# The last output product of a three-layer kernel, by token tiles instead of column blocks

## The chip, the cores and the metric

The kernel runs on one core of one Trainium2 chip. The metric is the device time of one execution in microseconds (us). TensorE multiplies matrices, VectorE and ScalarE do elementwise work, GpSimd helps with both, and SyncE issues the transfers. "Clock" below is the clock granted to TensorE.

## What is computed

A hidden state of 512 tokens x 1024 channels goes through a gated linear attention layer with an MLP, a differential attention layer with an MLP, and a third layer with two mixers side by side. The part that changes is the end of the third layer:

```python
y = jnp.einsum('bsc,cd->bsd', jnp.concatenate([o_a.astype(x.dtype), o_b], axis=-1), w_o[layer])
x = _layer_norm(DEEPNORM_ALPHA * x + y, ln_g[layer], ln_b[layer])

def _layer_norm(x, g, b):
    xf = x.astype(jnp.float32)
    mu = jnp.mean(xf, axis=-1, keepdims=True)
    var = jnp.mean(jnp.square(xf - mu), axis=-1, keepdims=True)
    y = (xf - mu) * lax.rsqrt(var + LN_EPS) * g.astype(jnp.float32) + b.astype(jnp.float32)
```

Here w_o is 1024 x 1024, the mean is over the 1024 channels of one token, and everything is float32. o_a comes from four attention heads (each gated by `a_gate`), o_b from four heads of a recurrence (gated by `b_gate`).

## The kernel before, in words

The state lives channel-major: `X[:, j, :]` holds channels 128j to 128j+127 on the partitions and all 512 tokens along the row. A product is split in two parts for accuracy: a value becomes a rounded high part and the rest, its low part (`Hh`/`Hl` for inputs, `Oh`/`Ol` for what goes into an output product, `Wh`/`Wl` for weights), and a product is three matmuls: high x high, low x high, high x low.

Weights stream through in 231 blocks, each 1024 inputs x 128 output columns, 512 KB. For each block b SyncE loads a raw tile (`weights`, three raw buffers, so b waits until the low part of b - 3 is done), ScalarE copies it rounded into a slot of `WH` (`w_hi`, line 1024 of the profile), VectorE subtracts (`w_lo`, line 1561), and TensorE runs 8 x 3 matmuls with the block as stationary and 512 tokens as moving operand (`add_k`, lines 483, 484, 486) into one PSUM bank. The blocks use three slots in turn; a block's copy waits for the product that last used its slot.

Each engine has one program in a fixed order. Around the change:

- Blocks 193 to 222 (`TWO` + n, n = 0 to 29) project the third layer's inputs. After block n each engine runs `two_tick(n)`, the steps of the attention heads and the recurrence that are due, up to n = 37. On TensorE, ticks 31 to 37 stand between the k steps of the output product. Lines of these ticks that matter here: 539 (transposes of 128 x 128), 942 (attention weights times values), 965 (value projection), 1113 to 1120 on ScalarE and 1648 on VectorE (the gate's silu), 2057 (gating of a head), 1103 and 1643 (high and low part of O).
- Blocks 223 to 230 (`TWO_WO` + j) are w_o. 223 and 224 are built together, one k after the other as the parts of O become ready (order `KORDER_2`: the recurrence's heads first), then the other six one by one. They alternate between PSUM banks 0 and 1.
- VectorE adds each block to the residual (line 2114), GpSimd sums the blocks over j (2206, 2209).
- Then the layer norm: mean by two products with a matrix of ones (lines 1003, 1005), centring on VectorE (2120), squares on ScalarE (1544), the variance by eight products with ones (1010), `rstd` on ScalarE (1047, 1049), scaling on VectorE (2123), bias on ScalarE (1548), and eight stores of 256 KB from SyncE (464).

`TB` and `G456` are rings of PSUM banks (2, 3 and 4, 5, 6); `take` hands out the next bank with the event that frees it. In `CB` lie the recurrence's states in this stage, in `con` the constants.

## Time and profile before

| | |
|---|---|
| median of 3 runs | 1589.82 us (1588.62 to 1593.27) |
| the profiled execution | 1588.16 us, of which the span of the records 1586.8 us |
| TensorE busy | 1533.2 us (97%), 7486 matmuls |
| VectorE, ScalarE, GpSimd busy | 993.5, 670.6, 174.1 us |
| mean granted clock | 0.99 of full |

"Busy" adds the records of an engine, so an engine that is busy 97% of the time is not the bound everywhere; the chain that ended last tells for each stretch who was waited for. The records of matmuls overlap: a matmul's duration is longer than the distance to the next one, and the distance (called pitch below) is what a stream of them costs. A few per cent of the matmul records can be missing.

### The profile page before, as it was taken

What the parts mean: (1) busy time and instruction counts of PE and PEld (TensorE: products, weight loads), DVE (VectorE), ACT (ScalarE), POOL (GpSimd) and SP (SyncE); (2) the same over time, 40 slices, a digit from 0 to 9 for tenths busy, and PEclk for the clock granted to TensorE, in tenths of its full rate; (3) what the DMA queues carried; (4) which work ended last, traced back from release to release, by engine and by line L of the source; (5) the groups of instructions that cost most, each with busy time, mean ns of one, the idle gap of its engine ahead of it and who ended that gap; (6) DMA issues with size and microseconds to landing.
All of it is one profiled execution on the core that took longest, in us unless ns stands there. A gap on an engine that the chain in (4) does not pass through costs nothing.

```text
span 1586.8 us, 18855 instructions
## 1 busy us (share of the span) xinstructions
PE 1533.2 (97%) x7486; PEld 1246.1 (79%) x7486; DVE 993.5 (63%) x1588; ACT 670.6 (42%) x1126; POOL 174.1 (11%) x160
## 2 busy tenths in 40 slices
PE   9999999999999999999988999999999999999997
PEld 6777878888888888777766878888888866887774
DVE  7476667866666655777774643434344569997743
ACT  6454434513232334465554532324133455555633
POOL 0000002000000001111102100000001003664110
PEclk9998999999999999999999999999999999999999
DMA  9234445565656542222212343333333122212111
GB/s 370 102 129 132 125 142 168 168 215 190 197 186 204 188 127 81 69 64 67 67 54 67 106 113 93 104 96 93 97 97 99 48 83 80 67 40 80 41 53 53
DMA packets 52172, 180.79 MB, mean 114 GB/s; under 512 B 5762, under 2 KB 6658, under 8 KB 52083
## 3 DMA queue, kind: packets, MB, share of 16 engines
q1 hardware_dynamic: 52082, 179.57, 36.0%
q8 instruction: 59, 0.97, 0.3%
q14 instruction: 31, 0.25, 0.0%
HBM read 176.01 MB, written 3.41 MB: 113 GB/s over the span
## 4 chain that ended last, share of the span: by engine, by line
PE 82%; DVE 8%; ACT 5%; POOL 2%; DMA 1%; issue 1%; SPq 1%; DVEq 0%; ACTq 0%
PE PS L483 22%; PE PS L486 22%; PE PS L484 22%; PE PS L493 2%; PE PS L494 2%; PE PS L496 2%; PE PS L720 1%; DVE sb_Wl L1561 1%; PE PS L539 1%; PE PS L869 1%; PE PS L739 1%; POOL sb_TMD L2194 1%; ACT sb_Wh L1024 1%; PE PS L633 1%; DMA sb_rg<-ada 1%
## 5 line engine op out<-in xcount | busy, mean ns | idle before, releaser
L483 PE MATMUL PS<-sb_Hh,sb_Wh 128*128 128x512 f32 (+1 forms) x1016 | 405.8, 399 | 2.3 <-DVE sb_Hl L1592 2.3
L486 PE MATMUL PS<-sb_Hh,sb_Wl 128*128 128x512 f32 (+1 forms) x1016 | 396.5, 390 | 0.6 <-DVE sb_Wl L1561 0.6
L484 PE MATMUL PS<-sb_Hl,sb_Wh 128*128 128x512 f32 (+1 forms) x1016 | 396.6, 390 | 0.0
L1024 ACT ACTIVATE sb_Wh<-sb_RAW 128x1024 fp32r<-128x1024 f32 x223 | 233.7, 1049 | 317.5 <-PE PS L486 310.1
L1561 DVE TENSOR_TENSOR sb_Wl<-sb_RAW,sb_Wh 128x1024 fp32r<-128x1024 f32 x223 | 282.2, 1266 | 94.0 <-ACT sb_Wh L1024 94.0
L483 PE MATMUL PS<-sb_Oh,sb_Wh 128*128 128x512 f32 x672 | 265.3, 395 | 5.5 <-DVE sb_X L1632 1.9
L486 PE MATMUL PS<-sb_Oh,sb_Wl 128*128 128x512 f32 x672 | 262.7, 391 | 2.7 <-DVE sb_Wl L1561 2.7
L484 PE MATMUL PS<-sb_Ol,sb_Wh 128*128 128x512 f32 x672 | 262.4, 391 | 0.0
L483 PEld LDWEIGHTS PS<-sb_Hh,sb_Wh 128*128 128x128 f32 (+1 forms) x1016 | 190.2, 187 | 59.1 <-issue 15.8
L486 PEld LDWEIGHTS PS<-sb_Hh,sb_Wl 128*128 128x128 f32 (+1 forms) x1016 | 190.2, 187 | 43.1 <-DVE sb_Wl L1561 1.0
L484 PEld LDWEIGHTS PS<-sb_Hl,sb_Wh 128*128 128x128 f32 (+1 forms) x1016 | 190.4, 187 | 39.9 <-issue 1.0
L1632 DVE SCALAR_TENSOR_TENSOR sb_X<-PS,sb_MOD,sb_X 128x512 f32<-128x512 f32 x76 | 57.0, 750 | 165.0 <-PE PS L486 165.0
L483 PEld LDWEIGHTS PS<-sb_Oh,sb_Wh 128*128 128x128 f32 x672 | 126.7, 189 | 33.7 <-ACT sb_Wh L1024 2.2
L486 PEld LDWEIGHTS PS<-sb_Oh,sb_Wl 128*128 128x128 f32 x672 | 126.7, 189 | 29.7 <-DVE sb_Wl L1561 3.2
L484 PEld LDWEIGHTS PS<-sb_Ol,sb_Wh 128*128 128x128 f32 x672 | 126.8, 189 | 26.6 <-issue 0.7
L2135 POOL TENSOR_TENSOR sb_SSQ<-sb_SSQ,sb_TMA 128x512 f32<-128x512 f32 x24 | 42.9, 1786 | 781.6 <-ACT sb_TMA L1039 781.6
L1792 DVE TENSOR_TENSOR sb_TMD<-sb_TMA 128x512 f32<-128x512 f32 x64 | 44.3, 692 | 121.3 <-ACT sb_TMA L1242 121.3
L1242 ACT ACTIVATE sb_TMA<-PS 128x512 f32<-128x512 f32 x64 | 38.1, 596 | 193.1 <-PE PS L486 188.0
L1568 DVE CUSTOM_DVE_ANT_0 sb_ARW<-sb_ARW,sb_CB,sb_vec 128x1024 f32<-128x1024 f32 x86 | 115.0, 1340 | 0.2
L1643 DVE TENSOR_TENSOR sb_Ol<-sb_TMD,sb_Oh 128x512 fp32r<-128x512 f32 x68 | 47.1, 693 | 2.9 <-DVE sb_TMD L1792 0.4
L1299 ACT ACTIVATE sb_WK<-PS,sb_st 128x512 f32<-128x512 f32 (+3 forms) x64 | 33.0, 525 | 33.1 <-DVE sb_st L1878 33.1
L493 PE MATMUL PS<-sb_Hh,sb_Wh 128*128 128x256 f32 x128 | 37.2, 290 | 6.3 <-DVE sb_Hl L1613 4.9
(355 smaller groups left out, 1942.7 us busy)
## 6 DMA issues: line engine op xcount, KB each, us to landing
sb_RAW<-w SPq DMA_DIRECT2D x128, 512.0 KB, 3.6
sb_ARW<-ada SPq DMA_DIRECT2D x86, 512.0 KB, 4.5
sb_RAW<-diff_in SPq DMA_DIRECT2D x24, 512.0 KB, 3.6
sb_RAW<-gla_in SPq DMA_DIRECT2D x20, 512.0 KB, 3.7
sb_RAW<-in_b SPq DMA_DIRECT2D x16, 512.0 KB, 4.0
sb_RAW<-gla_wo SPq DMA_DIRECT2D x8, 512.0 KB, 3.6
sb_RAW<-diff_wo SPq DMA_DIRECT2D x8, 512.0 KB, 3.6
sb_RAW<-wo SPq DMA_DIRECT2D x8, 512.0 KB, 3.6
```

What stands on the lines that cost most here:

```text
L483: mm(to[0:m, :], WH[si][:, k, 0:m], hi[:, k, :], start=first, stop=False)
L484: mm(to[0:m, :], WH[si][:, k, 0:m], lo[:, k, :], start=False, stop=False)
L486: ins = mm(to[0:m, :], WL[si][:, k, 0:m], hi[:, k, :], start=False, stop=last)
L493: mm(to, WH[si][:, k, :], hi[:, k, ts], start=k == 0, stop=False)
L1024: act(WH[slot_of(b)][:, :, 0:m], RAWS[raw_of(b)][:, 0:8 * m].rearrange("p (k m) -> p k m", k=8), ACT.Copy).then_inc(*done("w_hi", b))
L1242: act(to, bank(b), ACT.Relu).then_inc(*done("evac_a", b))
L1561: tt(WL[si][:, :, 0:m], RAWS[raw_of(b)][:, 0:8 * m].rearrange("p (k m) -> p k m", k=8), WH[si][:, :, 0:m].bitcast(F), ALU.subtract).then_i ...
L1568: e.op.tensor_tensor_reduce(w, w, CB[:], 1.0, V("ada_b", layer * 48 + t), ALU.mult, ALU.add, col).then_inc(*done("mod", layer, t))
L1632: stt(X[:, j, :], bank(b), gates_of[first][:, j:j + 1], X[:, j, :], ALU.mult, ALU.add).then_inc(*done("evac_d", b))
L1643: tt(Ol[:, k, :], src, Oh[:, k, :].bitcast(F), ALU.subtract).then_inc(*done("o_lo", stage, k))
L1792: tt(q, r, r, ALU.mult).then_inc(*done("m_sq", b))
L2135: tt(SSQ[:], SSQ[:], TA.buf(("sq", i, j)), ALU.add).then_inc(*done("ssq", i, j))
```

## The change

The last output product is computed token-major. For a tile i of 128 tokens and a half f of 512 output columns, a PSUM bank first gets the residual, by four transposes of `X`, and then 8 x 3 matmuls are added to it, with the tile's columns of `Oh`/`Ol` as stationary operand and four weight blocks (4 x 128 columns) as moving operand. (0, 0) and (1, 0) are built together between ticks 31 to 37, then (2, 0), (3, 0), (0, 1), (1, 1), (2, 1), (3, 1), each in a bank of its own. Since the residual isn't multiplied any more, O is divided by `ALPHA` instead, through the value weights and the recurrence's gain, and the norm's epsilon by its square.

All eight blocks of w_o are held at once: 223 to 225 in the three slots, 226 in a fourth slot over `CB` and the first 1024 columns of `con`, 227 to 230 over `Hh`/`Hl`. 226 is converted after block 221 (n = 28), 227 to 230 after the last tick.

The norm runs per token tile: VectorE takes statistics of each half (`bn_stats`), merges them, and makes two passes for each half; ScalarE computes the reciprocal root of one column. The gain and bias, now along the row, are loaded to all partitions. GpSimd has no part in it. Stores are 128 tokens x 512 columns. The output tensor is token-major.

```diff
@@ -155,16 +155,20 @@
+    if b >= TWO_WO + 3:
+        return b - TWO_WO + 6
     return THIRD.get(b, b if b < FIRST else (b - sum(b > n for n in THIRD)) % 3)
...
 BANKS[DIFF_WO + 2] = 4
-BANK = [BANKS.get(b, "turns" if b in THIRD or b in FOURTH else b % 2) for b in range(BLOCKS)]
+BANK = [BANKS.get(b, "turns" if b in THIRD or b in FOURTH else b % 2) for b in range(TWO_WO)]
 SLOT_BEFORE, BANK_BEFORE, NEXT_WEIGHTS = {}, {}, {}
-for _b in range(FIRST, BLOCKS):
+for _b in range(FIRST, TWO_WO + 3):
     SLOT_BEFORE[_b] = max(n for n in range(_b) if _b in THIRD or slot_of(n) == slot_of(_b))
-    BANK_BEFORE[_b] = max((n for n in range(_b) if BANK[n] == BANK[_b]), default=None)
+    if _b < TWO_WO:
+        BANK_BEFORE[_b] = max((n for n in range(_b) if BANK[n] == BANK[_b]), default=None)
@@ -249,22 +252,29 @@
-        Wh, Wl = sb("Wh", [P, 3, 8, 128], R), sb("Wl", [P, 3, 8, 128], R)
+        with ExitStack() as place:
+            Wh = sb("Wh", [P, 4, 8, 128], R, place)
+        sb("three_of_Wh", [P, 3072])
+        CB = sb("CB", [P, 1024])
+        with ExitStack() as place:
+            Wl = sb("Wl", [P, 4, 8, 128], R, place)
+        sb("three_of_Wl", [P, 3072])
+        con = sb("con", [P, NCON])
         RAW = sb("RAW", [P, 3, 1024])
         vec = sb("vec", [P, NVEC])
-        con = sb("con", [P, NCON])
         ones = sb("ones", [P, 128])
...
         epsb = sb("epsb", [P, 2])
-        CB = sb("CB", [P, 1024])
         relb = sb("relb", [32, 4])
...
         TMD = sb("TMD", [P, 2, T])
+        hgs = sb("hgs", [P, 4])
+        lst, lmv = sb("lst", [P, 4, 12]), sb("lmv", [P, 4, 4])
@@ -304,6 +314,8 @@
+        WH += [Wh[:, 3]] + [OV(Hh, n) for n in range(4)]
+        WL += [Wl[:, 3]] + [OV(Hl, n) for n in range(4)]
@@ -314,6 +326,8 @@
+        rows_bank = lambda i, f: [PS[:, 1, :], G456.buf(("out", 0, 1)), PS[:, 0, :], PS[:, 7, :], G456.buf(("out", 2, 0)),
+                                  TB.buf(("out", 2, 1)), G456.buf(("out", 3, 0)), TB.buf(("out", 3, 1))][2 * i + f]
@@ -350,6 +364,9 @@
+        TOK = [slice(i * 128, (i + 1) * 128) for i in range(4)]
+        LNG, LNB = SEL[:, 0:1024], MKP[:, 0:1024]
+        Y = [x[:, n:n + 2, :].rearrange("p a t -> p (a t)") for x in (Bc, SH) for n in (0, 2)]
@@ -457,12 +474,21 @@
-            for b in range(TWO_WO, BLOCKS):
+            for b in range(TWO_WO, TWO_WO + 2):
                 slot(b)
-            for j in range(8):
-                e.wait_ge(at("y", j))
-                e.op.dma_start(out[:, j, :], X[:, j, :]).then_inc(*landed("out", j))
-            e.wait_ge(at("out", 7))
+            e.wait_ge(at("a_max", 3, 0))
+            for n, to in enumerate((LNG, LNB)):
+                ap = D["ln"]
+                e.op.dma_start(to, bass.AP(tensor=ap.tensor, offset=ap.offset + n * 1024,
+                                           ap=[[0, 128], [1, 1024]])).then_inc(*landed("ln", n))
+            for b in range(TWO_WO + 2, BLOCKS):
+                slot(b)
+            for i in range(4):
+                for f in range(2):
+                    fs = slice(f * T, (f + 1) * T)
+                    e.wait_ge(at("y", i, f))
+                    e.op.dma_start(out[TOK[i], fs], Y[i][:, fs]).then_inc(*landed("out", i, f))
+            e.wait_ge(at("out", 3, 1))
@@ -961,7 +987,7 @@
-                    e.wait_ge(at("a_ol", h), at("wuv"), *free)
+                    e.wait_ge(at("a_ol", h), at("wuv_s"), *free)
@@ -993,21 +1019,39 @@
-            wo(TWO_WO, 7, lambda k: at("o_lo", TWO_WO, k), lambda n: two_tick(31 + n), KORDER_2)
-            for j in range(2, 8):
-                project(TWO_WO + j, (Oh, Ol))
-            to, free = TB.take("mean", ("cent", 7))
-            e.wait_ge(at("xsum", 6), *free)
-            mm(to, ones[:], SSQ[:], start=True, stop=False)
-            e.wait_ge(at("evac_d", TWO_WO + 7))
-            mm(to, ones[:], X[:, 7, :], start=False, stop=True).then_inc(*done("mean"))
-            to, free = TB.take("var", ("rstd", 5))
-            e.wait_ge(*free)
-            for j in range(8):
-                e.wait_ge(at("csq", j))
-                mm(to, ones[:], TA.buf(("csq", j)), start=j == 0, stop=j == 7).then_inc(*done("var", j))
+            def add_rows(i, f, k, first, last):
+                to, blocks = rows_bank(i, f), range(TWO_WO + 4 * f, TWO_WO + 4 * f + 4)
+                ks = slice(k % 4 * 128, k % 4 * 128 + 128)
+                wh, wl = (Hh[:, k // 4::2, ks], Hl[:, k // 4::2, ks]) if f else (Wh[:, :, k, :], Wl[:, :, k, :])
+                e.wait_ge(*(at("w_lo", b) for b in blocks))
+                if first:
+                    for j in range(4):
+                        mm(to[:, TOK[j]], X[:, 4 * f + j, TOK[i]], ident, start=j == 0, stop=False, is_transpose=True,
+                           skip_group_check=True)
+                mm(four(to), Oh[:, k, TOK[i]], wh, start=False, stop=False, skip_group_check=True)
+                mm(four(to), Ol[:, k, TOK[i]], wh, start=False, stop=False, skip_group_check=True)
+                ins = mm(four(to), Oh[:, k, TOK[i]], wl, start=False, stop=last, skip_group_check=True)
+                if last:
+                    ins.then_inc(*done("rows_out", i, f))
+            e.wait_ge(at(*evac(TWO_WO - 2)), at(*evac(TWO_WO - 1)))
+            for n, k in enumerate(KORDER_2):
+                e.wait_ge(at("o_lo", TWO_WO, k))
+                add_rows(0, 0, k, n == 0, n == 7)
+                add_rows(1, 0, k, n == 0, n == 7)
+                if n < 7:
+                    two_tick(31 + n)
+            for i, f in ((2, 0), (3, 0), (0, 1), (1, 1), (2, 1), (3, 1)):
+                if (i, f) == (1, 1):
+                    e.wait_ge(at("a_ol", 3))
+                else:
+                    to, free = (TB if f and i else G456).take(("out", i, f))
+                    e.wait_ge(*free)
+                for k in range(8):
+                    add_rows(i, f, k, k == 0, k == 7)
@@ -1019,7 +1063,11 @@
-                if b >= FIRST and b not in THIRD:
+                if b > TWO_WO + 3:
+                    e.wait_ge(at("proj", TWO_WO - 1))
+                elif b == TWO_WO + 3:
+                    e.wait_ge(at("r_o", 3))
+                elif b >= FIRST and b not in THIRD:
@@ -1379,6 +1427,9 @@
+            e.wait_ge(at("wuv"))
+            act(wuv[:], wuv[:], ACT.Copy, scale=1.0 / ALPHA).then_inc(*done("wuv_s"))
+            act(hgs[:], V("hg_g", 0, 4), ACT.Copy, scale=1.0 / ALPHA).then_inc(*done("hg_s"))
@@ -1532,20 +1583,19 @@
+                if n == 28:
+                    w_hi(TWO_WO + 3)
             for n in range(30, 38):
                 two_tick(n)
-            for b in range(TWO_WO, BLOCKS):
-                w_next(b)
-            for j in range(8):
-                to, free = TA.take(("csq", j), ("var", j))
-                e.wait_ge(at("cent", j), *free)
-                act(to, X[:, j, :], ACT.Square).then_inc(*done("csq", j))
-            rstd(TB.buf("var"), at("var", 7), RS[:], (5,), 1)
-            for j in range(8):
-                e.wait_ge(at("yg", j))
-                act(X[:, j, :], X[:, j, :], ACT.Identity, bias=V("ln_b", j)).then_inc(*done("y", j))
+            for b in range(TWO_WO + 4, BLOCKS):
+                w_hi(b)
+            for i in range(4):
+                e.wait_ge(at("ln_mv", i))
+                act(lmv[:, i, 2:3], lmv[:, i, 1:2], ACT.Ln, bias=epsb[:, 1:2]).then_inc(*done("rln", 5, i))
+                e.wait_ge(at("rln", 5, i))
+                act(lmv[:, i, 3:4], lmv[:, i, 2:3], ACT.Exp, scale=-0.5).then_inc(*done("rstd", 5, i))
@@ -1657,7 +1707,7 @@
-            e.op.memset(epsb[:, 1:2], LN_EPS).then_inc(*done("eps"))
+            e.op.memset(epsb[:, 1:2], LN_EPS / ALPHA ** 2).then_inc(*done("eps"))
@@ -2021,8 +2071,8 @@
-                    e.wait_ge(at("r_rs", h), at("r_on", h))
-                    stt(Q[:, h, :], TA.buf(("ron", h)), V("hg_g", h), TA.buf(("rsq", h)), ALU.mult,
+                    e.wait_ge(at("r_rs", h), at("r_on", h), at("hg_s"))
+                    stt(Q[:, h, :], TA.buf(("ron", h)), hgs[:, h:h + 1], TA.buf(("rsq", h)), ALU.mult,
@@ -2104,23 +2154,35 @@
+                if n == 28:
+                    w_lo(TWO_WO + 3)
                 for i, r in TOP.get(n, ()):
...
                 two_tick(n)
-            for j in range(8):
-                b = TWO_WO + j
-                e.wait_ge(at("proj", b))
-                stt(X[:, j, :], X[:, j, :], ALPHA, bank(b), ALU.mult, ALU.add).then_inc(*done("evac_d", b))
-                w_next(b)
-            e.wait_ge(at("mean"))
-            for j in range(8):
-                stt(X[:, j, :], TB.buf("mean"), -1.0 / 1024, X[:, j, :], ALU.mult, ALU.add).then_inc(*done("cent", j))
-            e.wait_ge(at("rstd", 5))
-            for j in range(8):
-                stt(X[:, j, :], X[:, j, :], V("ln_g", j), RS[:], ALU.mult, ALU.mult).then_inc(*done("yg", j))
+            for b in range(TWO_WO + 4, BLOCKS):
+                w_lo(b)
+            def ln_stats(i, f):
+                e.wait_ge(at("rows_out", i, f))
+                e.op.bn_stats(lst[:, i, 6 * f:6 * f + 6], rows_bank(i, f)).then_inc(*done("ln_st", i, f))
+            for i in range(4):
+                ln_stats(i, 0)
+            for i in range(4):
+                ln_stats(i, 1)
+                e.wait_ge(at("ln_st", i, 1))
+                e.op.bn_aggr(lmv[:, i, 0:2], lst[:, i, :]).then_inc(*done("ln_mv", i))
+                e.wait_ge(at("ln_mv", i), at("ln", 1))
+                for f in range(2):
+                    fs = slice(f * T, (f + 1) * T)
+                    stt(Y[i][:, fs], rows_bank(i, f), lmv[:, i, 0:1], LNG[:, fs], ALU.subtract,
+                        ALU.mult).then_inc(*done("ln_c", i, f))
+                for f in range(2):
+                    fs = slice(f * T, (f + 1) * T)
+                    e.wait_ge(at("rstd", 5, i), at("ln_c", i, f))
+                    stt(Y[i][:, fs], Y[i][:, fs], lmv[:, i, 3:4], LNB[:, fs], ALU.mult, ALU.add).then_inc(*done("y", i, f))
@@ -2200,13 +2262,6 @@
-            for j in range(7):
-                e.wait_ge(at("evac_d", TWO_WO + j))
-                if j == 0:
-                    e.op.tensor_copy(SSQ[:], X[:, 0, :]).then_inc(*done("xsum", 0))
-                else:
-                    e.wait_ge(at("xsum", j - 1))
-                    tt(SSQ[:], SSQ[:], X[:, j, :], ALU.add).then_inc(*done("xsum", j))
```

## Rows read from the trace of the kernel before

**Rows 1.** The page's section 4: the chain that ended last, by engine.

```profile
PE 82%; DVE 8%; ACT 5%; POOL 2%; DMA 1%; issue 1%; SPq 1%; DVEq 0%; ACTq 0%
```

**Rows 2.** The chain, last 20 us: start us, duration us, engine, tile, line, instructions.

```profile
1566.33 0.23 PE PS L486
...
1568.49 0.70 DVE sb_X L2120
...
1569.90 7.15 PE PS L1010 x16
...
1579.24 5.36 ACT sb_X L1548 x8
```

**Rows 3.** TensorE's timeline: start us, duration us, engine, line, operation, count.

```profile
1533.12 0.39 PE L486 MATMUL PS<-sb_Oh,sb_Wl 128*128 128x512 f32 x1
1533.61 0.50 PE L483 MATMUL PS<-sb_Oh,sb_Wh 128*128 128x512 f32 x1
...
1566.16 0.39 PE L486 MATMUL PS<-sb_Oh,sb_Wl 128*128 128x512 f32 x1
```

**Rows 4.** The same view, half-width matmuls; the 28th starts 27 steps later.

```profile
1245.73 0.28 PE L493 MATMUL PS<-sb_Hh,sb_Wh 128*128 128x256 f32 x1
...
1248.93 0.28 PE L493 MATMUL PS<-sb_Hh,sb_Wh 128*128 128x256 f32 x1
```

**Rows 5.** The same view, transposes (line 539) in the attention's ticks.

```profile
1499.50 0.60 PE L539 MATMUL PS<-sb_con,sb_SH 128*128 128x128 f32 x4
1499.94 0.49 PE L539 MATMUL PS<-sb_con,sb_vT 128*128 128x128 f32 x3
...
1508.39 0.30 PE L539 MATMUL PS<-sb_con,sb_vT 128*128 128x128 f32 x1
```

**Rows 6.** The chain from 1508 to 1520, columns as in group 2.

```profile
1508.76 1.83 PE PS L942 x14
...
1514.20 1.23 DVE sb_Wl L1561
...
1517.16 2.99 PE PS L942 x14
```

**Rows 7.** Timelines of ScalarE (ACT) and VectorE (DVE): [idle before, who ended it].

```profile
1258.02 0.60 ACT L1503 ACTIVATE sb_vT<-PS 128x512 f32<-128x512 f32 x1 [3.28 <-PE PS L496]
...
1504.17 1.04 ACT L1024 ACTIVATE sb_Wh<-sb_RAW 128x1024 fp32r<-128x1024 f32 x1
1506.59 0.60 ACT L1113 ACTIVATE sb_TMA<-PS 128x512 f32<-128x512 f32 x1 [1.37 <-PE PS L486]
...
1505.25 1.23 DVE L1561 TENSOR_TENSOR sb_Wl<-sb_RAW,sb_Wh 128x1024 fp32r<-128x1024 f32 x1 [0.26 <-ACT sb_Wh L1024]
1507.22 0.43 DVE L1648 TENSOR_SCALAR sb_TMA<-sb_TMA 128x512 f32<-128x512 f32 x1 [0.74 <-ACT sb_TMA L1113]
...
1526.73 0.69 DVE L1643 TENSOR_TENSOR sb_Ol<-sb_B,sb_Oh 128x512 fp32r<-128x512 f32 x1 [0.70 <-ACT sb_Oh L1103]
```

**Rows 8.** Groups by line, 1380 to the end: count, busy us, mean ns, idle before.

```profile
L2123 DVE SCALAR_TENSOR_TENSOR sb_X<-sb_X,sb_vec,sb_RS 128x512 f32<-128x512 f32 x8 | 5.4, 748 | 5.1 <-ACT sb_RS L1049 5.1
...
L2120 DVE SCALAR_TENSOR_TENSOR sb_X<-PS,sb_X 128x512 f32<-128x512 f32 x8 | 4.9, 682 | 1.2 <-PE PS L1005 1.2
...
L2025 DVE SCALAR_TENSOR_TENSOR sb_Q<-sb_TMA,sb_vec 128x512 f32<-128x512 f32 x4 | 3.8, 957 | 3.0 <-ACT sb_TMA L1058 3.0
...
L2044 DVE RECIPROCAL sb_st<-sb_st 128x1 f32<-128x1 f32 x16 | 2.6, 160 | 1.2 <-ACT sb_vT L1441 0.5
```

**Rows 9.** Transfers of the whole span: count, KB each, median us to landing.

```profile
sb_RAW<-wo SPq DMA_DIRECT2D x8, 512.0 KB, 3.6
...
yT<-sb_X SPq DMA_DIRECT2D x8, 256.0 KB, 2.2
```

**Rows 10.** Stretches: length; PE, PEld, DVE, ACT, POOL busy (count); clock; DMA share, GB/s.

```profile
1516.70:1518.00 1.30, 1.30 (x6) 1.30 (x7) 0.00 (x0) 0.80 (x3) 0.00 (x0) 0.50 0.69 258
```

More of the change, by code:

```diff
@@ L32 @@
        "ada_b": (40, 96), "b_a": (136, 4), "b_r": (140, 8), "gla_g": (148, 2), "sub_g": (150, 1),
-       "kv_g": (151, 1), "hg_g": (152, 4), "lb": (156, 8), "ln_g": (164, 8), "ln_b": (172, 8)}
-NVEC = 180
-CON = {"ident": (0, 128), "tri": (128, 128), "scan": (256, 512), "lev": (768, 7 * 128),
+       "kv_g": (151, 1), "hg_g": (152, 4), "lb": (156, 8)}
+NVEC = 164
+CON = {"scan": (0, 512), "lev": (512, 7 * 128), "ident": (1408, 128), "tri": (1536, 128),
        "adm": (1664, 128), "cau": (1792, 128), "freq": (1920, 1)}
@@ L185, in evac @@
     on_dve = (GLA <= b < GLA_WO and (b - GLA) % 6 in (2, 3)) or GLA_WO <= b < MLP0 or DIFF_WO <= b < MLP1
-    on_dve = on_dve or b >= TWO_WO
     for first in (MLP0, MLP1):
@@ L2262, in layout @@
              a["ada_b"], a["gla_b_a"], a["gla_b_r"], a["gla_norm_g"], a["diff_subln_g"], a["kv_norm_g_2"],
-             a["hgrn_norm_g_2"], a["lb_logits_2"], a["ln_g_2"], a["ln_b_2"]]
+             a["hgrn_norm_g_2"], a["lb_logits_2"]]
     d = {"con": con, "hot": hot, "vec": np.ascontiguousarray(np.concatenate([col(v) for v in parts], axis=1))}
@@ L2290, in layout @@
     d["wo_2"] = tiles(a["w_o_2"][0])
+    d["ln"] = np.concatenate([a["ln_g_2"], a["ln_b_2"]])
     return d
@@ L2300 @@
     D = {k: nc.dram_tensor(k, v.shape, mybir.dt.from_np(v.dtype), kind="ExternalInput").ap() for k, v in arrays.items()}
-    out = nc.dram_tensor("yT", (P, 8, T), F, kind="ExternalOutput").ap()
+    out = nc.dram_tensor("y", (T, 1024), F, kind="ExternalOutput").ap()
     build(nc, D, out)
     r = run_bass_kernel_spmd(nc, [arrays], core_ids=[0])
-    y = r.results[0]["yT"]
-    return np.ascontiguousarray(y.transpose(2, 1, 0)).reshape(1, T, 1024)
+    return np.ascontiguousarray(r.results[0]["y"]).reshape(1, T, 1024)
```

## The prediction

> **What bounds the kernel now.** I read the page first: the chain that ended last is 82% TensorE over the span [rows 1], so time is won only where TensorE's work shrinks or where it is not the bound. Then the chain of waits over the last 20 us [rows 2]. The last matmul of the output product ends at 1566.56 (1566.33 + 0.23), and the span at 1586.8. Between the two the reader is to see a strict relay over the whole 512 x 1024 result: VectorE's last residual and the mean, centring from 1568.49, squares and the variance sum on TensorE (7.15 us), two ScalarE steps, scaling on VectorE, the added bias on ScalarE in eight steps to 1584.60, then the last store. No other block's matmuls lie beside any of it. Before it, from 1533.61 to 1566.16, TensorE runs its last 144 matmuls at an even pitch [rows 3]: 143 steps in 32.55 us, 0.2276 us each. That stretch has nothing to give except by fewer matmuls. Last I looked at 1504 to 1521 [rows 6], because the change puts new work there.
>
> **The change part by part.** The sum goes by the end of the last product on TensorE, before at 1566.56 [rows 2].
>
> *The product itself.* Before: 8 column blocks x 8 k x 3 = 192 matmuls of 512 columns. After: 8 groups (token tile i, half f) x 8 k x 3 = 192 of 512 columns. Same count, with weights as the moving operand and O as the stationary one; each is still preceded by a 128 x 128 load. I take the pitch as unchanged, 0.2276 us, so 0. What the trace doesn't show is a moving operand in four pieces of 128 columns, 4 KB apart. The bound above: a 256-column matmul has a pitch of (1248.93 - 1245.73)/27 = 0.1185 us [rows 4], so, from 256 and 512 columns, a matmul is 0.426 ns a column and 0.0094 us of start; three more starts would be 0.028 us, x 192 = 5.4 us. Below: 0, since the same columns stream. I take 0: the pieces are contiguous inside and no instruction is added.
>
> *Transposes of the residual.* 32 are added, 4 a group, all in TensorE's dense stretch, so they count in full. The trace has the same operation (data stationary, identity moving): four start at 1499.50 and the next at 1499.94 [rows 5], 0.110 us each. 32 x 0.110 = +3.5 us. Upper end: 0.262 us, what a full float32 matmul of 128 columns costs (14 records, two a matmul, in 1.83 us [rows 6]), so 8.4 us. I take 3.5, as it is the same operation.
> A single transposition's record is 0.27 us or more long although the next starts 0.11 us later. The Trainium skill, in "TensorE: Matmul & The Clock Gate", Part 4: PE-mode transpose, gives about 275 ns for one in a kernel's context; by that, as a price, an estimate of 32 x 0.275 = 8.8 us. The trace has the record's length but contradicts it as a pitch.
>
> *A small stall goes.* Before, block 225 waits for the residual of 223 to leave its bank: the matmul at 1533.12 is followed only at 1533.61 [rows 3], 0.49 instead of 0.23 us. Eight groups now have eight banks. -0.3 us.
>
> *Weights earlier.* The first group needs blocks 223 to 226 converted, not 223 and 224. 225 is ready at 1515.43 [rows 6]. 226 is new there: its copy goes on ScalarE behind the one that starts at 1504.17, into the 1.37 us in which ScalarE waits for TensorE [rows 7], and takes 1.05, so it is covered (its raw tile is asked for when 223's low part is done, a block earlier, and lands in 3.6 [rows 9]). Its subtraction goes on VectorE behind 1505.25 + 1.23 and takes 1.23 to about 1507.6; the gap there ended at 1507.22 [rows 7]. So the step of line 1648 and, right behind it in VectorE's queue, the gating of head 0 (L2057) slip by about 0.3 us. TensorE waits for that gating: its bank is the one the transposition at 1508.39 takes [rows 5]. Behind it everything to 1516.7 is a chain [rows 6], so +0.3 us. If the cover on ScalarE were gone it would be +1.05. TensorE's product starts near 1520 (1517.16 + 2.99 [rows 6]), so the four-block wait itself costs 0, with 4 us to spare.
> Blocks 227 to 230 wait for H to be free and sit on both queues behind the last low part of O, at 1526.73 [rows 7]. Four copies of 1.05, subtractions of 1.23, and one transfer of 3.6 (230's raw buffer frees with 227): ready near 1537. The first half-1 group starts near 1546. Covered by 9 us of matmuls.
>
> *SyncE.* The two 512 KB loads of the norm's vectors stand in its queue before 228's tile, behind a wait for the last attention row minimum, which in VectorE's queue lies ahead of the subtraction at 1505.25 [rows 7]. A 512 KB tile lands in 3.6 us [rows 9], but these two repeat one source row for all partitions, which I have no row for at this size; they are wanted near 1552, so they could take ten times as long. Cost 0.
>
> *ScalarE, GpSimd.* The two scalings (value weights, gain) stand once before 1258, where ScalarE waits 3.28 us for TensorE [rows 7]: 0.8 us, covered. GpSimd's seven sums and ScalarE's sixteen passes over X go; they cost the path only within the tail.
>
> *The norm of tiles 0 to 2.* Per tile VectorE has two statistics, one aggregation and four 128 x 512 passes: 2 x 0.69 + 0.2 + 4 x 0.67 = 4.3 us against a group's 24 x 0.2276 + 0.44 = 5.9 us. Hidden; it would not be if a tile took over 5.9. (Statistics of half 0 are done earlier still.)
>
> *The new tail*, after the last product: statistics of a 128 x 512 PSUM bank. No row shows that instruction; nearest is line 2120 with PSUM input, 0.68 [rows 8]. Bounds 0.43 (line 1648, a one-input pass [rows 7]) and 1.36 (two passes). I take 0.7. Aggregation: 0.2, near the 0.16 of a one-column reciprocal plus a self-wait [rows 8]; bounds 0.1 and 0.4. Two passes from PSUM: first 0.61 to the next (4.9/8), and 0.61 again before the dependent one. ScalarE's two one-column steps run beside them. Two passes from SBUF: 0.67 + 0.75 [rows 8]. Sum 0.7 + 0.2 + 1.2 + 1.4 = 3.5 us. Then the store: last ScalarE step ended 1584.60, span end 1586.8, so 2.2 us, and the landing is 2.2 [rows 2, 9].
>
> *Sum.* 1566.6 + 3.5 - 0.3 + 0.3 = 1570.1 for the last product; + 3.5 + 2.2 = 1575.8 against 1586.8: 11.0 us less. The tail after the product goes from 20.2 to 5.7 us (-14.5), and 3.5 of that is given back on TensorE. The profiled execution took 1588.16 and would take 1577.2. The median of the three runs shown is 1589.82, 1.66 above it, so 1578.8 on the median's scale, which is my number.
>
> **Rivals.** *A. Costlier matmuls in pieces.* Each gap in the moving operand costs a start: +5.4 us, 1584.2. For: no row has such an operand. Against: the price is for a whole instruction's start. *B. Costlier transposes.* 0.262 us each, +4.9 us: 1583.7. For: they alternate with another data mode in each group. Against: [rows 5]. *C. The clock moves.* After TensorE's wait for the steps of that chain, to 1516.7, the granted clock was 0.50 (1.2 of 2.4 GHz) and the 14 records took 2.99 us instead of 1.83 [rows 6, 10]. The gap stays, but shifted by 0.3 us; the low stretch may be missed (-1.2, 1577.6) or be as much longer (+1.2, 1580.0). It stays within the forecast's own range. *D. The tail isn't hidden, the change does less than it says.* If the statistics take 1.36 us and the passes 0.96 (the mean of line 2025, the same kind of pass [rows 8]), a tile takes 2.72 + 0.2 + 3.84 = 6.8 us, above 5.9; three tiles lag 2.7 us, and the last one is 0.66 + 4 x 0.29 = 1.8 longer: +4.5, 1583.3. For: passes of other stages are that slow. Against: those of the tail are not, and GpSimd is idle there now. *E. Slower.* Each 128-column piece runs as a matmul of its own at the price of [rows 6], 0.131 us: a matmul takes 0.52 and the product gains 0.30 x 192 = 57 us, 1636. It lies in the pitch of the 192; the kernel is slower once that passes 0.2276 + 11.0/192 = 0.285 us. For: the same lack of a row. Against: it needs TensorE to end its stream at each piece.
>
> **How the numbers follow.** Forecast with C 0.66; A 0.09, B 0.08, D 0.06; E or some price like it 0.05; the rest, 0.06, is a mix of A, B and D, which would come out from 1585 up. The forecast's own spread is about 3 us, of which 1.6 is how a median stands to one execution. Range 1575 to 1585, which takes in C, A, B and D and leaves out mixes and E. A measurement of this kernel can tell about 0.3%, 4.8 us, from no change: faster is below 1585.05. A, B and D lie within 1.4 us of that, so 0.05 of their 0.23 goes to "within"; of the mixes 0.04 are within and 0.02 above 1594.6. So faster 0.66 + 0.18 = 0.84, within 0.3% 0.05 + 0.04 = 0.09, slower 0.05 + 0.02 = 0.07.
>
> **What would show it.** Right: the 192 matmuls keep a pitch of 0.227 us; groups of four transposes take 0.44 us; TensorE's last product ends 3.5 us later than before, about 1570; VectorE idles ahead of each group's statistics; 5.7 us lie between the last product and the end; and 1508 to 1516 is shifted by 0.3 us. Wrong: a pitch above 0.23 (A, E); over 0.15 us a transposition (B); VectorE without idle time between tiles (D); TensorE waiting for a low part of weights near 1519 or 1546; or a slow load of the norm's vectors holding VectorE near 1552.

## The result, and the profile after

The changed kernel took 1577.10 us as the median of 7 runs (1571.00 to 1582.87) against 1589.82 for the kernel before (1585.01 to 1593.46 in 7): a ratio of 0.9927, with a 95% interval of 0.9906 to 0.9947. It was measured again beside the last experiments: 1580.34 of 12 runs against 1587.96 of 17, 0.9955 [0.9935, 0.9976]. Both intervals lie below 1; the first is wholly beyond the 0.3% that can be told from no change, the second reaches to 0.24%. So the kernel is faster, and the size of the gain is known less well, 12.7 us once and 7.6 us once. The profiled execution took 1577.1 us with a span of 1575.8, 11.0 less than before.

The page's section 4, the chain that ended last by engine, answers [rows 1]:

```profile
PE 84%; DVE 7%; ACT 4%; POOL 2%; issue 1%; DMA 1%; SPq 0%; DVEq 0%; ACTq 0%
```

TensorE holds two points more of the chain. The chain itself, from 1508 us on, answers [rows 2, 6]; its columns are start, duration, engine, tile, line and count:

```profile
1508.74 0.30 PE PS L565
1509.04 1.63 PE PS L968 x14
1510.67 0.45 PE PS L565 x4
...
1516.76 0.47 PE PS L565
1517.24 2.94 PE PS L968 x14
1520.17 0.44 PE PS L1032 x4
...
1534.41 0.44 PE PS L1032 x4
...
1564.01 0.44 PE PS L1032 x4
...
1569.72 0.24 PE PS L1036
1569.98 0.71 DVE sb_lst L2169
...
1570.96 0.81 DVE sb_SH L2180 x2
1571.77 0.52 issue
1572.28 1.40 DVE sb_SH L2185 x2
```

Line 1032 is the group of four transposes at the head of each group of matmuls. Five groups lie between 1534.41 and 1564.01, so a group takes 5.92 us: 0.44 for the transposes and 24 x 0.228 for the matmuls. The last product ends at 1569.96 (1569.72 + 0.24), and 5.84 us lie between that and the end, where 20.2 lay before. VectorE's timeline shows the norm of one tile and the head of the next, with the idle time ahead of it in brackets:

```profile
1558.14 0.70 DVE L2169 BATCH_NORM_STATS2 sb_lst<-PS 128x6 f32<-128x512 f32 x1 [2.22 <-PE PS L1036]
1558.87 0.21 DVE L2176 BATCH_NORM_AGGREGATE sb_lmv<-sb_lst 128x2 f32<-128x12 f32 x1
1559.11 1.41 DVE L2180 SCALAR_TENSOR_TENSOR sb_B<-PS,sb_lmv,sb_SEL 128x512 f32<-128x512 f32 x2
1560.44 1.40 DVE L2185 SCALAR_TENSOR_TENSOR sb_B<-sb_B,sb_lmv,sb_MK 128x512 f32<-128x512 f32 x2
...
1564.05 0.70 DVE L2169 BATCH_NORM_STATS2 sb_lst<-PS 128x6 f32<-128x512 f32 x1 [2.21 <-PE PS L1036]
```

A tile's norm takes 3.7 us (1558.14 to 1561.84), and VectorE then waits 2.21 us for TensorE to finish the next group. So it is hidden.

### The profile page after: what moved, and what is told of

Read it like the earlier page. It is cut to its first block, busy times and chain, and to the rows that moved or that the text cites. A ratio compares the mean times of both kernels' runs of the same rounds, so it can differ in the third digit from the quotient of the medians.

```text
span 1575.8 us, 18857 instructions
## 1 busy us (share of the span) xinstructions
PE 1527.8 (97%) x7498; PEld 1246.3 (79%) x7498; DVE 992.3 (63%) x1592; ACT 661.8 (42%) x1118; POOL 164.9 (10%) x153
## 3 DMA queue, kind: packets, MB, share of 16 engines
HBM read 177.05 MB, written 3.41 MB: 115 GB/s over the span
## 4 chain that ended last, share of the span: by engine, by line
PE 84%; DVE 7%; ACT 4%; POOL 2%; issue 1%; DMA 1%; SPq 0%; DVEq 0%; ACTq 0%
PE PS L509 22%; PE PS L512 21%; PE PS L510 21%; PE PS L519 2%; PE PS L520 2%; PE PS L522 2%; PE PS L895 1%; PE PS L746 1%; PE PS L565 1%; DVE sb_Wl L1611 1%; PE PS L765 1%; POOL sb_TMD L2256 1%; PE PS L1036 1%; PE PS L1034 1%; PE PS L1035 1%
## 5 line engine op out<-in xcount | busy, mean ns | idle before, releaser
L1072 ACT ACTIVATE sb_Wh<-sb_RAW 128x1024 fp32r<-128x1024 f32 x219 | 229.3, 1048 | 297.8 <-PE PS L512 290.6
L1611 DVE TENSOR_TENSOR sb_Wl<-sb_RAW,sb_Wh 128x1024 fp32r<-128x1024 f32 x219 | 274.9, 1256 | 92.1 <-ACT sb_Wh L1072 92.1
L509 PE MATMUL PS<-sb_Oh,sb_Wh 128*128 128x512 f32 x608 | 239.6, 394 | 5.4 <-DVE sb_X L1682 1.8
L512 PE MATMUL PS<-sb_Oh,sb_Wl 128*128 128x512 f32 x608 | 237.9, 391 | 2.7 <-DVE sb_Wl L1611 2.7
L510 PE MATMUL PS<-sb_Ol,sb_Wh 128*128 128x512 f32 x608 | 237.4, 391 | 0.0
L509 PEld LDWEIGHTS PS<-sb_Oh,sb_Wh 128*128 128x128 f32 x608 | 114.7, 189 | 30.6 <-ACT sb_Wh L1072 2.2
L512 PEld LDWEIGHTS PS<-sb_Oh,sb_Wl 128*128 128x128 f32 x608 | 114.6, 189 | 27.3 <-DVE sb_Wl L1611 3.2
L510 PEld LDWEIGHTS PS<-sb_Ol,sb_Wh 128*128 128x128 f32 x608 | 114.8, 189 | 23.9 <-issue 0.5
```

The costliest lines, as they stand in the source:

```text
L509: mm(to[0:m, :], WH[si][:, k, 0:m], hi[:, k, :], start=first, stop=False)
L510: mm(to[0:m, :], WH[si][:, k, 0:m], lo[:, k, :], start=False, stop=False)
L512: ins = mm(to[0:m, :], WL[si][:, k, 0:m], hi[:, k, :], start=False, stop=last)
L1072: act(WH[slot_of(b)][:, :, 0:m], RAWS[raw_of(b)][:, 0:8 * m].rearrange("p (k m) -> p k m", k=8), ACT.Copy).then_inc(*done("w_hi", b))
L1611: tt(WL[si][:, :, 0:m], RAWS[raw_of(b)][:, 0:8 * m].rearrange("p (k m) -> p k m", k=8), WH[si][:, :, 0:m].bitcast(F), ALU.subtract).then_i ...
```

## The experiments

All edits are made to the changed kernel. The value projection of head 0 (line 991, before 965) starts anywhere from 1501.40 to 1513.54 us in the traces of kernels in which nothing that TensorE does before it differs. So I take it as a mark, and the experiments are read by the distance from the start of that projection to the end of the last product on TensorE, within one trace. It is 60.17 us before the change (1506.39 to 1566.56) and 63.50 after it (1506.46 to 1569.96); the second trace of the changed kernel gives 63.59, so the distance repeats within 0.1 us. The tail behind the product is read separately. With its tail the changed kernel needs 69.34 us from the mark to the end (69.46 in its second trace) where the kernel before needs 80.41: 11 us less, which is a better measure of the change than one whole time.

How early the mark comes goes with the mean granted clock of the execution: 1501.40 us at 0.996 (the kernel with the doubled transposes below) and 1513.54 at 0.989 (the second trace of the changed kernel). So whole times of single executions can't rank these kernels. Doubled transposes took 1575.53 us in all and the run with block 226 later 1574.14, both less than the changed kernel's 1577.10, although both have more in their way.

**The norm behind the whole product.** The overlap of norm and product is undone and all else kept: before its last four half-1 statistics VectorE waits for the last group.

```diff
+            e.wait_ge(at("rows_out", 3, 1))
             for i in range(4):
                 ln_stats(i, 1)
```

> The changed kernel, but VectorE waits for the very last product before it finishes the norm of any tile (statistics of half 0 are still taken early). Theory (the gain is the overlap of three tiles' norms with the products): per tile 0.7 us of statistics, 0.2 of aggregation and about 2.7 of passes, 3.6 us, of which three tiles now stand behind the last product: the last product ends at about 1570 as before, and 10.7 us more lie behind it, so the span is about 1586.5 and the gain is gone. Rival (the gain is that the token-major norm needs fewer and cheaper steps, with no ones-products): the span stays near 1576 to 1578.

The distance was 63.60 us, as in the changed kernel, and the tail 16.7 us instead of 5.84: +10.9. VectorE's timeline has the idle time in one piece, and then one tile every 3.63 us:

```profile
1576.92 0.70 DVE L2169 BATCH_NORM_STATS2 sb_lst<-PS 128x6 f32<-128x512 f32 x1 [22.99 <-PE PS L1036]
...
1580.55 0.69 DVE L2169 BATCH_NORM_STATS2 sb_lst<-PS 128x6 f32<-128x512 f32 x1
...
1590.07 1.41 DVE L2186 SCALAR_TENSOR_TENSOR sb_SH<-sb_SH,sb_lmv,sb_MK 128x512 f32<-128x512 f32 x2
```

10.9 is three tiles at 3.63 us. From the mark to the end it is 80.3 us (1513.30 to 1593.6), and in the kernel before 80.4 (1506.39 to 1586.8): the new form of the norm alone gives no more than the transposes take, and the gain is the overlap with the product, which the order by token tiles allows. (The whole time of this execution was 1594.88 us.)

**The transposes twice.** Each group of four is issued twice; the second writes the same values to the same places.

```diff
                 if first:
+                  for _ in range(2):
                     for j in range(4):
```

> The changed kernel with each group's four transposes made twice, the second set over the first. Theory (a transposition costs 0.110 us of TensorE): 32 more are +3.5 us, the last product ends at about 1573.5 and the span at 1579.3. Rival B (0.262 us each): +8.4 us, span 1584.2.

```profile
1555.69 0.87 PE PS L1033 x8
...
1562.05 0.87 PE PS L1033 x8
```

The chain has eight in 0.87 us, twice the 0.44 of four. The distance was 66.99: +3.49 us for 32 transposes, 0.109 each (+3.40 and 0.106 against the changed kernel's second trace). The row of before [rows 5] gave their price, and rival B is out. The Trainium skill's 275 ns ("TensorE: Matmul & The Clock Gate", Part 4: PE-mode transpose) is again the length of one record (0.30 in the chain above), not what one more transposition costs.

**The pieces of the moving operand.** The four pieces of 128 contiguous columns of a matmul's moving operand are replaced by 512 columns a fixed distance apart, at the same number of columns and instructions. They are other columns of the weights, so the product isn't the layer's. First 32 bytes apart:

```diff
-                wh, wl = (Hh[:, k // 4::2, ks], Hl[:, k // 4::2, ks]) if f else (Wh[:, :, k, :], Wl[:, :, k, :])
+                apart = lambda x, s: x.rearrange(s)[:, k::8].rearrange("p (a b) -> p a b", a=4)
...
```

> The changed kernel with the moving operand's 512 columns taken 32 bytes apart from each other instead of in four contiguous pieces of 512 bytes. It multiplies other weight columns than the reference's, so its output is not the layer's; work and order are the same. Theory (pieces cost nothing as long as the same number of columns streams): the pitch stays 0.227 us and the span 1576. Rival A (what isn't contiguous costs TensorE's read): 512 pieces instead of 4 make each matmul slower; at twice the pitch the 192 matmuls take 43.5 us more, span 1619.

Two later runs put them 8 bytes apart (two columns in 16 bytes), as here, and 16 bytes apart (one), in the same way with 2048 and 4 in place of 1024 and 2:

```diff
-                apart = lambda x, s: x.rearrange(s)[:, k::8].rearrange("p (a b) -> p a b", a=4)
+                apart = lambda x, s: x.rearrange(s)[:, k // 2 * 1024 + k % 2:(k // 2 + 1) * 1024:2].rearrange("p (a b) -> p a b", a=4)
```

> As moving_apart (other weight columns than the reference's, same work and order), with the moving columns 8 bytes apart, two in every 16 bytes. Theory (the read goes by 16-byte lines and is at full speed from two columns a line on): pitch 0.227 us, the first value projection to the last product 63.5 us. Rival (whatever isn't adjacent costs half): 0.43 us, about 102 us as with 32 bytes.

> As moving_apart, with the moving columns 16 bytes apart, one in every 16 bytes. Theory (one column a line, as with 32 bytes): pitch 0.43 us, the same measure about 102 us. Rival (the price grows with the distance): between 0.227 and 0.43 us.

TensorE's timeline at 32, 8 and 16 bytes, two neighbouring matmuls each; the difference of the starts is the pitch:

```profile
1552.50 0.62 PE L1038 MATMUL PS<-sb_Wl,sb_Oh 128*128 128x512 f32 x1
1552.93 0.62 PE L1036 MATMUL PS<-sb_Wh,sb_Oh 128*128 128x512 f32 x1
```

```profile
1550.21 0.65 PE L1038 MATMUL PS<-sb_Wl,sb_Oh 128*128 128x512 f32 x1
1550.66 0.65 PE L1036 MATMUL PS<-sb_Wh,sb_Oh 128*128 128x512 f32 x1
```

```profile
1549.91 0.66 PE L1038 MATMUL PS<-sb_Wl,sb_Oh 128*128 128x512 f32 x1
1550.37 0.66 PE L1036 MATMUL PS<-sb_Wh,sb_Oh 128*128 128x512 f32 x1
```

The pitch was 0.43 us at 32 bytes, 0.45 at 8 and 0.46 at 16, against 0.228 for the pieces, at a granted clock of 1.00 in all of them. The distances were 101.9, 106.2 and 108.3 us: 38 to 45 us for 192 matmuls, and whole times of 1611.18, 1623.84 and 1620.80. The theory was wrong at 32 and at 8 bytes, where I had expected no cost. So the layout of the moving operand can double the price of a matmul, but three gaps between contiguous pieces that start 4 KB apart cost nothing. The Trainium skill ("Advanced Engine Details and Errata", SBUF Cachelines) asks for at least two accesses to the same 16 bytes to take up the latency of the memory. Were two enough, columns of this type 8 bytes apart would be free, and the run shows that they aren't here: 8 bytes cost about as much as 16 and 32. These runs separate adjacent from non-adjacent columns. Why it is so, and how short a piece may be, they don't show.

**Block 226 a step later.** The copy and the subtraction of weight block 226 go one block back, behind those of 225, which leaves SyncE's order and all else as it is.

```diff
-                if n == 28:
+                if n == 29:
                     w_hi(TWO_WO + 3)
...
-                if n == 28:
+                if n == 29:
                     w_lo(TWO_WO + 3)
```

> The changed kernel with block 226's copy and subtraction one block later, behind those of 225, on both engines. Theory (the stretch 1508 to 1516.7 is one chain over ScalarE and VectorE that ends in TensorE's idle time, and 226 sits in a free place of it now): the subtraction of 226 comes ahead of the gating of head 1, which TensorE waits for, so TensorE's first product starts 1.1 to 1.3 us later, and the end too; the small shift of 0.07 us at 1508 goes. Rival (the weights have 4 us to spare, wherever they are): no change, 0.0 us.

```profile
1509.11 0.96 ACT sb_Wh L1072
...
1510.09 2.36 DVE sb_Wl L1611 x2
1512.45 0.60 DVE sb_Ol L1693
1513.05 0.61 DVE sb_B L2107
...
1513.70 0.36 PE PS L565
```

The chain now has two subtractions (2.36 us instead of 1.23) ahead of the low part of O and of the gating (line 2107) for which TensorE waits. The second copy isn't in the chain: ScalarE makes it beside the first subtraction. TensorE's timeline gives the wait as 4.09 us, where the changed kernel has 2.96: +1.13. The distance was 64.74: +1.24 us. The other 0.11 lies behind the wait, where the first group's transposes now fall under the low clock (0.61 us instead of 0.44). Where 226 stands decides what it costs: here a subtraction, there nothing that can be seen. (The shift of 0.07 us in the expectation was none; see the slip below.)

**Three ways to shorten that idle time.** It is the last one on TensorE before the product, and a chain sets it: ScalarE's copy of block 225, its subtraction, the low part of O for head 0, the gating of head 1. In the trace above the granted clock is 0.50 (1.2 GHz) from the end of this idle time until about 1520. Three edits attack it, the first alone, the second on top of the first, the third alone, and then all together.

The copy of 225 goes ahead of the two copies of attention weights that ScalarE makes last in that tick (line 1498), its subtraction ahead of VectorE's last product of the silu (line 2135):

```diff
+                        if n == 29 and a == 3:
+                            w_hi(TWO_WO + 2)
                         att_step(a, step)
...
+                        if n == 29 and kind == "ga":
+                            w_lo(TWO_WO + 2)
```

> The changed kernel with block 225 converted earlier: its copy on ScalarE ahead of the last two attention copies of tick 29 (ScalarE idles 1.3 us there), its subtraction on VectorE ahead of the silu product of that tick (idle 2.1 us there). Measured from the value projection of head 0 to the end of the last product, 63.50 us in the changed kernel. Theory (TensorE's 2.96 us of idle time hangs on the chain copy of 225, subtraction of 225, low part of head 0, gating of head 1): the chain is about 1.5 us shorter, so 62.0, and 60.8 if the clock then doesn't fall for the 14 records behind it. Rival (another release is as late, a copy of attention weights or the silu): within 0.3 us of 63.5.

Then VectorE also gates head 1 before it makes the low part of head 0:

```diff
+                if n == 30:
+                    tasks[0], tasks[1] = tasks[1], tasks[0]
```

> As w225_early, and VectorE gates head 1 before it makes the low part of head 0. Theory: TensorE's idle time ends another 0.5 us earlier, 61.4 us on the same measure, 60.2 if the clock stays up. Rival: the low part of head 0 then holds something else, and it is 62 as before.

And TensorE makes the transposes of the first two groups within the idle time, in front of the transposition that waits for the gating:

```diff
                     att_turn(h, 1)
+                    if h == 3:
+                        e.wait_ge(at(*evac(TWO_WO - 2)), at(*evac(TWO_WO - 1)))
+                        turn_rows(0, 0)
+                        turn_rows(1, 0)
                     att_turn(h, 0)
```

> The changed kernel with the eight transposes of the first two groups moved into TensorE's idle time, ahead of the transposition that waits for the gating of head 1. Theory (they need only X and two banks that are free by then): 8 x 0.109 = 0.87 us leave the path, 62.6 on the same measure, and the idle time shrinks from 2.96 to 2.1 us. Whether the clock still falls behind it isn't foreseen: 61.4 if it doesn't. Rival (they delay the waiting transposition or the chain behind it): 63.5.

> 225 early, gating of head 1 first, and the eight transposes in the idle time. Theory: the parts add up as far as the idle time reaches, 63.5 - 2.1 - 0.9 = 60.5, and 59.3 with the clock up. Rival (the parts compete for one gap, the last of them is worth nothing): 61.4 or more.

TensorE's timeline, the transposition behind the idle time, in the first (with the first transposes of the product), the second and the third edit:

```profile
1518.35 0.33 PE L565 MATMUL PS<-sb_con,sb_Q 128*128 128x128 f32 x1 [1.48 <-DVE sb_B L2110]
...
1520.08 0.60 PE L1032 MATMUL PS<-sb_con,sb_X 128*128 128x128 f32 x4
```

```profile
1518.08 0.33 PE L565 MATMUL PS<-sb_con,sb_Q 128*128 128x128 f32 x1 [0.87 <-DVE sb_B L2110]
```

```profile
1516.28 0.33 PE L565 MATMUL PS<-sb_con,sb_Q 128*128 128x128 f32 x1 [2.09 <-DVE sb_B L2113]
...
1518.86 0.63 PE L1042 MATMUL PS<-sb_Wh,sb_Ol 128*128 128x512 f32 x1
1519.29 0.63 PE L1043 MATMUL PS<-sb_Wl,sb_Oh 128*128 128x512 f32 x1
```

The stretches behind it, by window (length; PE, PEld, DVE, ACT, POOL busy with counts; granted clock; DMA share, GB/s), for the first and the third:

```profile
1518.40:1520.00 1.60, 1.60 (x15) 1.60 (x16) 0.46 (x1) 1.28 (x3) 0.00 (x0) 1.00 0.84 341
```

```profile
1516.30:1518.00 1.70, 1.70 (x13) 1.70 (x14) 0.52 (x1) 1.32 (x4) 0.00 (x0) 0.87 0.82 258
1518.00:1519.00 1.00, 1.00 (x5) 0.90 (x5) 0.51 (x2) 1.00 (x2) 0.00 (x0) 0.50 1.01 414
```

| kernel | idle, us | low clock (0.50), from the idle time's end | distance, us | against the changed kernel |
|---|---|---|---|---|
| block 226 later | 4.09 | from 0.2 us on | 64.74 | +1.24 |
| changed kernel | 2.96 | at once | 63.50 | |
| the same, second trace | 2.96 | from 1.2 us on | 63.59 | +0.09 |
| transposes ahead | 2.09 | from 1.3 us on | 62.72 | -0.78 |
| block 225 ahead | 1.48 | none | 60.50 | -3.00 |
| with head 1's gating first | 0.87 | none | 59.88 | -3.62 |
| all three | none | none | 58.96 | -4.54 |

The first edit took 1.48 us from the idle time but 3.00 from the distance. The other 1.52 is the clock, which stayed at 1.00: from the transposition behind the idle time to the product's first transposes the changed kernel takes 3.41 us (1516.76 to 1520.17 in its chain), and this one, with the same work, 1.89 (1518.35 to 1520.24 in its chain). The third took 0.87 us of work out of the product and moved it into the idle time, and the clock fell all the same, only later. In the changed kernel's first trace the low stretch covers the transposition and the 14 records; here it covers the product's first matmuls, with a pitch of 0.43 us. The changed kernel's second trace has it as late as here, and against that one the third edit gained 0.87 us.

Each of these low stretches lasted 3.4 us. One came at the end of this idle time in all ten traces in which it was 2.09 us or longer, and in none of the four in which it was 1.48, 0.87 or nothing (one trace each, two with all three edits). So at this place the shorter idle time and the clock go together in every trace. It isn't a rule by the length of one wait: some 10 us ahead of the mark TensorE waits 0.90 and 0.82 us in two places close together, and a low stretch followed there in the second edit's trace (granted clock 0.50 from 1501.00 to 1504.30), while in the changed kernel's first trace, with the same waits, it stayed at 1.00.

With all three, TensorE's timeline has no idle time between the matmuls of the attention and the product:

```profile
1511.09 1.04 PE L946 MATMUL PS<-sb_con,sb_X 128*128 128x128 f32 x8
1512.13 0.33 PE L565 MATMUL PS<-sb_con,sb_Q 128*128 128x128 f32 x1
...
1513.78 0.48 PE L1041 MATMUL PS<-sb_Wh,sb_Oh 128*128 128x512 f32 x1
```

**The changed kernel and the one with all three edits, timed side by side.**

> The changed kernel again, on the same chip as all_three_timed. Theory: ratio to before 0.993, as in the first measurement (11 us of 1588).

> The three edits together, timed. Theory (on one execution 58.96 us from the first value projection to the last product instead of 63.50): 4.5 us less than the changed kernel on the same chip, a ratio of 0.990 to before against 0.993. Rival (what was won there is lost in the executions' spread or in another stage): the same ratio as after_timed.

With the three edits the median was 1572.10 us of 6 runs (1566.61 to 1576.72), 0.9906 [0.9872, 0.9939] of the kernel before; the changed kernel's on the same chip was 1580.34, 0.9955 [0.9935, 0.9976]. By the medians it beats both; the two intervals overlap slightly. Against the changed kernel the medians say 8.2 us and the traces' distances 4.5 to 4.6 (58.96 in both of its traces, 63.50 and 63.59). I take 4.5 for the gain. The rest goes with the clock ahead of the mark: three of its six executions had a mean granted clock of 0.996 or more, and none of the changed kernel's twelve was above 0.994.

## Why the prediction was right

The forecast was 1578.8 us, and 1577.2 for the profiled execution, which took 1577.1. Its mechanism is what the runs show: the tail shrinks because three of four tiles are normed under the product, and part of that is given back for the transposes. By its steps:

- *The pitch of the product*, 0: right. The five equal groups show it: (5.92 - 0.44)/24 = 0.228 us, at most 0.1 us more over 192 matmuls.
- *The transposes*, +3.5: right. Four take 0.44 us, and doubling them cost 3.49.
- *The stall at 1533* [rows 3], -0.3: gone. There is no gap in the chain there. The distance is 3.33 us longer, and 3.49 - 0.26 leaves 0.1. That isn't the slip (next point); it lies in the product itself.
- *The slip*, +0.3: this step was wrong; measured from the mark it is 0.00. TensorE's last idle time before the product ends 10.30 us behind the mark before the change (1516.69 - 1506.39) and 10.30 after it (1516.76 - 1506.46); the 0.07 by which it is later is there at the mark already. The gating of head 0 did come later, by 0.35 us (its record starts at 1507.91 instead of 1507.56), and so did TensorE's transposition, 1508.74 instead of 1508.39 [rows 5]; of that 0.28 is left when the mark's 0.07 is taken off. But behind the transposition come the 14 records of line 942 [rows 6], and before the change these didn't wait for it last. The chain of before shows for what:

```profile
1508.12 0.60 ACT sb_FB L1464
1508.72 0.04 issue
...
1510.59 0.45 PE PS L539 x4
```

 ScalarE's copy of head 1's result out of its bank (line 1464), which doesn't hang on the gating, released them at 1508.72. TensorE's timelines, before and after, show how the transposition's delay is swallowed:

```profile
1508.39 0.30 PE L539 MATMUL PS<-sb_con,sb_vT 128*128 128x128 f32 x1
1508.76 1.16 PE L942 MATMUL PS<-sb_vT,sb_ctok 128*128 128x128 f32 x8
...
1510.43 0.60 PE L539 MATMUL PS<-sb_con,sb_SH 128*128 128x128 f32 x4
```

```profile
1508.74 0.30 PE L565 MATMUL PS<-sb_con,sb_vT 128*128 128x128 f32 x1 [0.37 <-DVE sb_B L2107]
1508.87 1.12 PE L968 MATMUL PS<-sb_vT,sb_ctok 128*128 128x128 f32 x8
...
1510.51 0.60 PE L565 MATMUL PS<-sb_con,sb_SH 128*128 128x128 f32 x4
```

 The first of the 14 starts 0.37 us behind the transposition before the change and 0.13 behind it after, so it is 0.11 later, and the next transposes are 0.08 later, 0.01 from the mark. (That the chain gives the 14 records 1.63 us after and 1.83 before is mostly the overlap with the record in front of them, which the chain counts there.) The run with block 226 later confirms it: there the gating starts 1.17 us behind the mark, as before the change (1.45 in the changed kernel), and the value projection of head 1 starts 5.33 us behind it in both, 5.32 before. The failing step reads "Behind it everything to 1516.7 is a chain": that was true of the copy's path and not of the gating's, which had about 0.3 us to spare. I had taken a wait of TensorE's for the one that set the pace, though the chain of before goes through another.
- *Block 226 on ScalarE*: covered. ScalarE makes both copies back to back from 1504.22 (1.99 us), and its next work, at 1506.66, still waits 0.45 us for TensorE, where 1.37 had been idle [rows 7]. No run took this cover away: with 226 later ScalarE's second copy was hidden too, and what cost was VectorE's subtraction.
- *Blocks 227 to 230*: the last low part is ready at 1535.81, predicted near 1537; the first half-1 group starts at 1546.25, predicted near 1546. Cost 0, with 10 us to spare.
- *The norm's vectors*: no cost, as predicted. The page's list of DMA issues gives the time from issue to landing, which no row of before had:

```profile
sb_SEL<-ln SPq DMA_DIRECT2D x1, 512.0 KB, 5.4
sb_MK<-ln SPq DMA_DIRECT2D x1, 512.0 KB, 6.1
```

 They are slower than the 3.6 us of a weight tile of the same size [rows 9], issued at 1506.92 and 1507.39, and wanted only near 1552. They were under way together, right behind a weight tile. Whether the repeated row or the other transfers made them slower isn't shown.
- *The norm of tiles 0 to 2*: hidden, with 2.2 us to spare in each group.
- *The new tail*, 5.7: measured 5.84. Statistics 0.70 and aggregation 0.21 as taken; the two passes from PSUM 1.32 to the start of the next (1570.96 to 1572.28) instead of 1.2, since one takes 0.75 and not the 0.68 of line 2120 [rows 8]; the two from SBUF 1.40; so 3.7 instead of 3.5, and 2.1 for the store.

The slip was 0.3 too dear, the product 0.1 too cheap and the tail 0.14 too cheap. They nearly cancel, and that part of the agreement is luck; without it the forecast would still have been within 0.3 us of the trace. A larger piece of luck is that the two profiled executions reach the mark within 0.07 us of each other, 1506.39 and 1506.46, while other traces of the same work lie up to 7 us later and 5 earlier. The 11 us less between mark and end don't hang on that; the 0.1 us of agreement in the whole time does. On the median's scale I had added 1.66 us; the first measurement's median was equal to its profiled execution, so that term was scatter of the runs, and the second measurement, 1580.34, lies on the other side of the forecast.

Of the rivals, B (dearer transposes) and D (the norm not hidden) are refuted by the rows above. C was not there in the profiled execution: the low stretch starts and ends where it did, its 14 records taking 2.94 us instead of 2.99. In the changed kernel's second trace the stretch did move, by 1.2 us, and cost 0.09 and not 1.2: it was as long, and only other work fell into it. A and E are refuted for this operand; the runs with separated columns show that TensorE does have such a price, far above A's 0.028 us a matmul. The price of an instruction's start, taken from [rows 4], was no measure for a gap in the operand.

## What to carry to other kernels

A closing step that needs a whole row of the result pays to be cut into tiles when the product can be reordered to finish one row tile at a time; check first that a tile's step is shorter than a tile's product, and charge what the new order adds to the engine that is the bound. When a step is put in front of a wait, ask which of the waits behind it ends last: look for another input of the same work before you charge the slip. When a matmul's operands change roles, look at how the moving columns lie; contiguous pieces of 128 were free here, columns apart doubled the price.

## What the runs showed of the hardware

- Moving columns that aren't adjacent, at 8, 16 and 32 bytes, raise a matmul of 512 columns from 0.228 us to 0.45, 0.46 and 0.43. That 8 bytes are no cheaper than 32 I had not expected.
- After TensorE had been idle for 0.87 and 1.48 us in front of the product the granted clock stayed at 1.00 (2.4 GHz); after 2.09, 2.96 and 4.09 us it was 0.50 (1.2 GHz) for 3.4 us, and this stretch began with the end of the idle time in some traces and 1.1 to 1.4 us later in others, the same kernel among both. Eight transposes inside the idle time didn't prevent it while 2.09 us of idleness were left behind them. Shortening the idle time to 1.48 us returned twice what was cut.
- The same waits of 0.90 and 0.82 us were followed by such a stretch in one trace and by none in another, and executions with a mean granted clock of 0.996 came to the same point of the program up to 12 us earlier than one with 0.989.
- Two loads of 512 KB that repeat one source row for all 128 partitions landed in 5.4 and 6.1 us, against 3.6 for a plain tile; they were under way at the same time.
